# Values of the last 16 tokens: plain fp32 products in four column groups in place of tiles of three products

## The reference

```python
h = jnp.concatenate([meta, x], axis=1)              # 16 + 512 = 528 tokens
xn = rms_norm(h, norm_gains[layer, 0])
proj = xn @ w_in[layer]                             # 528 x 1024 times 1024 x PROJ_WIDTH, fp32
q_a, k_a, v_a, f_a, q_b, k_b, v_b, g_a, g_b = jnp.split(proj, SPLIT_POINTS, axis=-1)
log_f = jax.nn.log_sigmoid((f_a + b_forget[layer]).astype(jnp.float32))
o_a = forgetting_attention(_split_heads(q_a, 8), _split_heads(k_a, 8), _split_heads(v_a, 8),
                           log_f.transpose(0, 2, 1))
o_b = stick_breaking_attention(_split_heads(q_b, 8), _split_heads(k_b, 8), _split_heads(v_b, 8))
y_a = _merge_heads(o_a) @ w_o_fox[layer]            # then gates, w_out, the FFN and a second block
```

## Time and profile before

| | value |
|---|---|
| median of 3 runs | 1541.97 us |
| profiled execution, its own time | 1542.34 us |
| its span (first to last instruction) | 1540.5 us |
| PE busy | 1492.9 us, 97% of the span |
| PEld busy | 1319.4 us, 86% |
| DVE busy | 1025.0 us, 67% |
| ACT busy | 655.0 us, 43% |
| mean granted TensorE clock | 0.993 |
| loads of 1 MB on SP's queue, issue to landing, median | 4.8 us |

### The profile page before, as it was taken

One profiled execution on the slowest core, in us unless ns is written; L12 is line 12 of the kernel. 1 busy time (PEld: TensorE's weight loads), 2 busy tenths in 40 slices (PEclk: granted clock), 3 DMA queues, 4 the chain that ended last, 5 costly groups with the idle time before them and its releaser, 6 DMA issues.

```text
span 1540.5 us, 27902 instructions
## 1 busy us (share of the span) xinstructions
PE 1492.9 (97%) x11772; PEld 1319.4 (86%) x11772; DVE 1025.0 (67%) x1441; ACT 655.0 (43%) x1052; POOL 23.3 (2%) x20
## 2 busy tenths in 40 slices
PE   7999999999998999999999899999989999999998
PEld 7989878889998999999777667768667999998876
DVE  5533447875446977777665766676688888885454
ACT  5433443443334222212343555446645555554343
POOL 0000000000000000000000011000000000000000
PEclk9999999999998999999999999999999999999999
DMA  5222004443222323322344213110113233222222
GB/s 183 83 83 83 16 21 161 148 160 109 105 101 74 115 103 120 121 103 101 133 149 150 92 50 110 55 35 29 35 48 110 83 110 110 106 94 79 93 96 82
DMA packets 37707, 147.74 MB, mean 96 GB/s; under 512 B 4304, under 2 KB 4432, under 8 KB 27856
## 3 DMA queue, kind: packets, MB, share of 16 engines
q1 hardware_dynamic: 36288, 142.76, 26.8%
q10 hardware_dynamic: 1152, 2.16, 0.4%
q0 software_dynamic: 144, 1.05, 0.2%
HBM read 143.86 MB, written 2.10 MB: 95 GB/s over the span
## 4 chain that ended last, share of the span: by engine, by line
PE 83%; DVE 9%; ACT 5%; issue 2%; DMA 1%; POOL 0%; ACTq 0%; DVEq 0%
PE ps L567 19%; PE ps L569 18%; PE ps L568 18%; PE ps L1488 4%; PE ps L1486 4%; PE ps L1487 4%; ACT t L1539 2%; DVE t L2264 1%; PE ps L603 1%; PE ps L604 1%; PE ps L605 1%; PE ps L751 1%; PE ps L1192 1%; PE ps L729 1%; PE ps L1161 1%
## 5 line engine op out<-in xcount | busy, mean ns | idle before, releaser
L567 PE MATMUL ps<-t 128*128 128x258 f32 (+4 forms) x2160 | 689.0, 319 | 21.9 <-DVE t L2312 8.6
L569 PE MATMUL ps<-t 128*128 128x258 f32 (+4 forms) x2160 | 677.4, 314 | 0.0
L568 PE MATMUL ps<-t 128*128 128x258 f32 (+4 forms) x2160 | 676.2, 313 | 0.0
L567 PEld LDWEIGHTS ps<-t 128*128 128x128 f32 (+1 forms) x2160 | 407.6, 189 | 66.0 <-issue 16.0
L569 PEld LDWEIGHTS ps<-t 128*128 128x128 f32 (+1 forms) x2160 | 407.3, 189 | 27.2
L568 PEld LDWEIGHTS ps<-t 128*128 128x128 f32 (+1 forms) x2160 | 408.3, 189 | 23.8
L2264 DVE TENSOR_TENSOR t<-t 128x1024 fp32r<-128x1024 f32 (+2 forms) x121 | 205.8, 1700 | 203.8 <-ACT t L1539 203.8
L1539 ACT ACTIVATE t<-t 128x1024 fp32r<-128x1024 f32 (+2 forms) x121 | 174.0, 1438 | 186.0 <-PE ps L569 173.4
L1488 PE MATMUL ps<-t 128*128 128x256 f32 x504 | 142.6, 283 | 0.0
L1486 PE MATMUL ps<-t 128*128 128x256 f32 x504 | 142.5, 283 | 0.1
L1487 PE MATMUL ps<-t 128*128 128x256 f32 x504 | 141.3, 280 | 0.0
(11 more groups left out here) (322 smaller groups left out, 1771.5 us busy)
## 6 DMA issues: line engine op xcount, KB each, us to landing
t<-in_W SPq DMA_DIRECT2D x75, 1024.0 KB, 4.8
t<-in_W SPq DMA_DIRECT2D x62, 512.0 KB, 3.2
t<-in_W SPq DMA_DIRECT2D x100, 256.0 KB, 3.5
t<-in_W SPq DMA_DIRECT2D x4, 644.0 KB, 3.8
t<-in_XT ACTq DMA_DIRECT2D x8, 264.0 KB, 7.8
out<-t SPq DMA_DIRECT2D x8, 256.0 KB, 2.7
t<-in_ROPE POOLq DMA_DIRECT2D x1, 1024.0 KB, 5.3
t<-in_CONS SPq DMA_DIRECT2D x1, 423.0 KB, 11.7
```

Source lines behind the costliest of these rows:

```text
L567: pe.matmul(out, wh, xh, start=first, stop=False)
L568: pe.matmul(out, wh, xl, start=False, stop=False)
L569: return pe.matmul(out, wl, xh, start=False, stop=last)
```

## The change

The last 16 tokens' values leave the tiles of three. For each pair of chunks (va 0 and 1, vb 0 and 1) one step `v_ends` makes all 512 columns with plain fp32 matmuls from the raw weights in `wraw`: for each of 8 contraction blocks four matmuls of 128 columns, each into another group of 32 PSUM partitions (rows 0, 32, 64, 96; 16 rows used) of bank 0. That is 32 matmuls with a 128x16 stationary operand instead of 2 x 24 matmuls of 256 columns. The stationary operand `xend` is a new fp32 tile, high plus low of those tokens, made by one DVE addition. DVE copies the result out with four copies of 16x128 instead of two of 16x256.

`v_ends` needs both raw chunks of the pair at once, so it stands fifth of nine steps: tiles 0 to 3 of the first chunk, `v_ends`, tiles 0 to 3 of the second. SP's loads into the two slots now also wait for it (`RAW_USED`): qb 0 and qb 1 wait for va's, ga 0 and woa 0 for vb's. `FILL_A` has a filler less of vb, and fills the place by cutting the first qb tile into its two parts, steps 0 and 1; the others come a step later. vb's `v_ends` is in step 13, and vb 1's first tile, with ga 0's split, in step 14.

```diff
@@ tables @@
-                   ("mm_v", 5, [("va", 0), ("va", 1), ("vb", 0), ("vb", 1)]),
+for _i, _c in enumerate(("va", "vb")):
+    USED[_c, 0], USED[_c, 1] = ("mm_v", 9 * _i + 4), ("mm_v", 9 * _i + 9)
+RAW_USED = {(_c, _i): 9 * _p + 5 for _p, _c in enumerate(("va", "vb")) for _i in range(2)}
-FILL_A = [("qb", 0, 0), ("qb", 0, 1), ("qb", 1, 0), ("qb", 1, 1), ("kb", 0, 0), ("kb", 0, 1), ("kb", 1, 0), ("kb", 1, 1)]
-FILL_A += [("vb", _i, _t) for _i in range(2) for _t in range(5)]
+FILL_A = [("qb", 0, 0, (0,)), ("qb", 0, 0, (1,)), ("qb", 0, 1, (0, 1)), ("qb", 1, 0, (0, 1)), ("qb", 1, 1, (0, 1))]
+FILL_A += [("kb", _c, _i, (0, 1)) for _c in range(2) for _i in range(2)]
+FILL_A += [("vb", 0 if _at < 5 else 1, _at, ()) for _at in range(9)]
+def chunk_starts(f):
+    name, c, i, parts = FILL_A[f]
+    return i in (0, 5) if name == "vb" else i == 0 and parts[0] == 0
@@ build @@
+        xend = sb(s_fox, [P, 8, 16])
@@ SP, weights @@
+                if n >= 2 and ORDER[n - 2] in RAW_USED:
+                    sp_.wait_ge(S["mm_v"], RAW_USED[ORDER[n - 2]])
@@ PE @@
-            for c in range(2):
-                w = weights(AT["va", c], 8)
-                for t in range(5):
-                    v_tile(c, t, w, min(128, T1 - 128 * t), 2 * c if t % 2 else 0,
-                           0 if t % 2 else (3 * c + 1 if t == 4 else 3 * c))
+            def v_ends(name):
+                pe.wait_ge(S["f_d"], 1)
+                for n in (AT[name, 0], AT[name, 1]):
+                    pe.wait_ge(S[f"d_w{n % 2}"], 16 * (n // 2 + 1))
+                for k in range(8):
+                    for g in range(4):
+                        at = 256 * k + 128 * (g % 2)
+                        ins = pe.matmul(bank(0, 128, slice(32 * g, 32 * g + 16)), xend[:, k, :],
+                                        wraw[:, AT[name, g // 2] % 2, at:at + 128], start=(k == 0), stop=(k == 7),
+                                        skip_group_check=True)
+                ins.then_inc(S["mm_v"], 1)
+            def v_step(pair, i):
+                nonlocal w
+                name = ("va", "vb")[pair]
+                if i in (0, 5):
+                    w = weights(AT[name, i // 5], 8)
+                if i >= 4:
+                    e = i - 4
+                    pe.wait_ge(S["ev_v_a" if e % 2 else "ev_v_d"], 4 * pair + e // 2 + 1 if e % 2 else
+                               6 * pair + (1, 2, 4)[e // 2])
+                if i == 4:
+                    v_ends(name)
+                else:
+                    tokens(w, i - i // 5 * 5, T1, P, i % 4).then_inc(S["mm_v"], 1)
+            for i in range(9):
+                v_step(0, i)
@@ ACT (DVE alike: split at i == 5, evac_v by steps) @@
-            for c in range(2):
-                split(AT["va", c] + 1)
-                for t in range(5):
-                    evac_v(c, t)
+            split(AT["va", 0] + 1)
+            for i in range(9):
+                if i == 5:
+                    split(AT["va", 1] + 1)
+                evac_v(0, i)
@@ DVE @@
+            dv.wait_ge(S["xl"], 16)
+            dv.tensor_tensor(xend[:, :, :], xnh[:, :, T2:T1].bitcast(F), xnl[:, :, T2:T1].bitcast(F), ALU.add
+                             ).then_inc(S["f_d"], 1)
+                if i == 4:
+                    for g in range(4):
+                        ins = dv.tensor_copy(dst[0:16, 4, 128 * g:128 * g + 128], bank(0, 128, slice(32 * g, 32 * g + 16)))
+                        if g % 2:
+                            ins.then_inc(S["ev_v_d"], 1)
...
```

More of the change, by code:

```diff
@@ L182, with qk_of @@
 XH0 = (8, 16, 32, 40)
-FILL_A = [("qb", 0, 0), ("qb", 0, 1), ("qb", 1, 0), ("qb", 1, 1), ("kb", 0, 0), ("kb", 0, 1), ("kb", 1, 0), ("kb", 1, 1)]
-FILL_A += [("vb", _i, _t) for _i in range(2) for _t in range(5)]
+FILL_A = [("qb", 0, 0, (0,)), ("qb", 0, 0, (1,)), ("qb", 0, 1, (0, 1)), ("qb", 1, 0, (0, 1)), ("qb", 1, 1, (0, 1))]
[4 more added lines that the diff above has]
+    return i in (0, 5) if name == "vb" else i == 0 and parts[0] == 0
+def qk_of(f):
+    name, c, i, _ = FILL_A[f]
+    return (8 if name == "qb" else 12) + 2 * c + i
 def evac_b(f):
@@ L660, in _, with qk_tile @@
                         ins.then_inc(S["mm_qk"], 1)
-            def qk_tile(g, w):
+            def qk_tile(g, w, parts=(0, 1)):
                 if g < 8:
@@ L669, in qk_tile @@
                         pe.wait_ge(S["ev_qk_a"] if g % 2 else S["ev_qk_d"], g // 2 - 4 if g % 2 else 4 + g // 2)
-                    tile(w, g % 2, 128, 8, xnh, xnl, 0, H2, 2 * (g % 2)).then_inc(S["mm_qk"], 1)
+                    for q in parts:
+                        ins = tile(w, g % 2, 128, 8, xnh, xnl, 264 * q, H2[q:q + 1], 2 * (g % 2) + q)
+                    if 1 in parts:
+                        ins.then_inc(S["mm_qk"], 1)
             w = weights(1, 8)
@@ L708, in fox_scores @@
                     pe.wait_ge(S["ev_qk_d"], 8)
-                    pe.wait_ge(S["f_d"], 3)
+                    pe.wait_ge(S["f_d"], 4)
                     pe.wait_ge(S["cst"], 9)
@@ L792, in fill_a @@
                 nonlocal w
-                name, c, i = FILL_A[f]
-                if i == 0:
-                    w = weights(AT[name, c], 8)
[L796 to L806, removed]
+                name, c, i, parts = FILL_A[f]
+                if name == "vb":
+                    if i == 0:
+                        pe.wait_ge(S["ev_qk_d"], 12)
+                    if i == 2:
+                        pe.wait_ge(S["ev_qk_a"], 4)
+                    v_step(1, i)
+                    return
+                if chunk_starts(f):
+                    w = weights(AT[name, c], 8)
+                if f == 0:
+                    pe.wait_ge(S["ev_v_d"], 6)
+                    pe.wait_ge(S["ev_v_a"], 4)
+                qk_tile(qk_of(f), w, parts)
             for n in range(20):
@@ L1638, in evac_qk, with evac_v @@
                               ).then_inc(S["ev_qk_a"], 1)
-            def evac_v(c, t):
-                if t % 2 == 0:
+            def evac_v(pair, i):
+                if i % 2 == 0:
                     return
[L1644 to L1647, removed]
+                t, col = i - i // 5 * 5, 256 * (i // 5)
+                ac.wait_ge(S["mm_v"], 9 * pair + i + 1)
+                ac.activation((va, vb)[pair][:, t, col:col + 256], bank(i % 4, 256), ACT.Copy).then_inc(S["ev_v_a"], 1)
             split(AT["f", 0] + 1)
@@ L1661, in _ @@
             ac.wait_ge(S["cst"], 1)
-            ac.wait_ge(S["f_d"], 2)
+            ac.wait_ge(S["f_d"], 3)
             ac.activation(ct[0:8, :], cs, ACT.Copy).then_inc(S["f_a"], 1)
-            for c in range(2):
-                split(AT["va", c] + 1)
-                for t in range(5):
-                    evac_v(c, t)
+            split(AT["va", 0] + 1)
[3 more added lines that the diff above has]
+                evac_v(0, i)
             def fox_exp(n):
@@ L1707, in fill_a @@
             def fill_a(f, part):
-                name, c, i = FILL_A[f]
+                name, c, i, parts = FILL_A[f]
                 if part == 0:
-                    if i == 0:
+                    if chunk_starts(f):
                         split(AT[name, c] + 1)
                 elif name == "vb":
-                    evac_v(2 + c, i)
-                else:
-                    evac_qk(8 + f)
+                    evac_v(1, i)
+                elif 1 in parts:
+                    evac_qk(qk_of(f))
             for n in range(20):
@@ L2332, in norm0, with evac_v @@
                 norm_tiles(0, 0, T1, lambda k: h[:, k, :], lambda k: V("g0", k), None, xnh, xnl, k0, k1)
-            def evac_v(c, t):
-                if t % 2:
+            def evac_v(pair, i):
+                if i % 2:
                     return
-                dst, col, m = (va, 256 * c, min(P, T1 - 128 * t)) if c < 2 else (vb, 256 * (c - 2), min(P, T1 - 128 * t))
-                dv.wait_ge(S["mm_v"], 5 * c + t + 1)
-                dv.tensor_copy(dst[0:m, t, col:col + 256], bank(t % 4, 256, slice(0, m))).then_inc(S["ev_v_d"], 1)
+                dst, t, col = (va, vb)[pair], i - i // 5 * 5, 256 * (i // 5)
+                dv.wait_ge(S["mm_v"], 9 * pair + i + 1)
+                if i == 4:
[3 more added lines that the diff above has]
+                            ins.then_inc(S["ev_v_d"], 1)
+                else:
+                    dv.tensor_copy(dst[:, t, col:col + 256], bank(i % 4, 256)).then_inc(S["ev_v_d"], 1)
             dv.wait_ge(S["rst"], 1)
@@ L2359, in _ @@
                                     ).then_inc(S["f_d"], 1)
-            dv.wait_ge(S["f_d"], 1)
+            dv.wait_ge(S["f_d"], 2)
             dv.tensor_tensor_scan(cs, cf, cf, 0.0, ALU.add, ALU.bypass).then_inc(S["f_d"], 1)
@@ L2409, in fill_a @@
             def fill_a(f, part):
-                name, c, i = FILL_A[f]
+                name, c, i, parts = FILL_A[f]
                 if part == 0:
-                    if i == 0:
+                    if chunk_starts(f):
                         split(AT[name, c] + 1)
```

(6 more changed lines are left out.)

6 lines of the change are left out of this document (removed).

## The result

The changed kernel takes 1537.79 us in the median of 6 runs (1535.6 to 1538.13), before 1542.12 beside it (6 runs, 1541.25 to 1542.56). The ratio is 0.9971 with an interval of 0.9961 to 0.9982: 4.3 us less, where 6.35 were forecast. The profiled execution took 1538.07 us, its span is 1536.3.

A forecast was written before the change was run, and what follows sets the result against it. PE, busy for 97% of the span, was taken to bound the kernel. 4.55 us from the va stretch plus 1.8 from the fox loop, 6.35 in all, gave 1535.6 us as median, range 1533.2 to 1539.8.

The forecast's parts named there:

- likeliest case: `v_ends` runs four abreast, with new waits between 0 and 3 us; 1533.7 to 1537, chance 0.73.
- What goes: 16-token tiles cost as much as full ones: two of 5.6 us in va, two fillers of 5.94 in the fox loop.
- the va stretch: PE from the first va tile to the first fox scores, 29.45 us: 4.55 us go, qb 0's load stays covered.
- `v_ends`: 32 plain fp32 matmuls on PE, four abreast: 2.05 us each time with switches, in va and in fox step 13.
- fox scores row: Trace of four 512-column matmuls, each in its own column group: 0.22 us a set of four at 128 columns.
- two abreast: Rival: 128 rows feed no more than two streams, `v_ends` takes 4.0 us; 1538.9 in all, chance 0.12.
- one after the other: Slower rival: `v_ends`' column groups run serially, 7.6 us each time; 1546.1 in all, chance 0.05.
- The fox loop: Two fillers out, one `v_ends` and a switch in: 3.7 us less 1.9 of new waits gives 1.8.
- sum of waits: New PE waits in fox steps 13 and 14: 0.45, 0.2, 0.95 and 0.3, together 1.9 us.
- Everything behind is only moved: All after the fox loop keeps its length and comes some 6.4 us earlier.
- The late load: Rival: ga 0's load lands beyond 4.7 us, delaying step 14; 1538.9 at 8 us, 1542.6 at 11.7; chance 0.08.
- none of the new waits: Rival: the close races in steps 13 and 14 cause no waits; 1533.7; no chance of its own given.

The follow-up runs named there:

- e_vb_only: Against the kernel before: `v_ends` for vb alone, va's tiles as before; 1540.92 us, ratio 0.9995.
- e_late_split: Against the changed kernel: the split of ga 0 on ACT and DVE moved from step 14 to step 15; 1535.35 us.
- e_vb_early: Against the changed kernel: vb's `v_ends` in the third of its nine places, fox step 11 instead of 13; 1534.28 us, run again 1535.70.
- the repeat: The changed kernel run once more, unaltered; 1537.88 us, ratio 0.9974 to the kernel before.
- e_two_groups: Against the changed kernel: `v_ends` writes to two column groups and two halves of each instead of four groups; 1542.70 us.
- e_one_group: Against the changed kernel: `v_ends` writes all four quarters to one column group, at four offsets in the bank; 1549.64 us.

## Why the prediction was right, and where it was not

**The direction, the mechanism and the range held.** 1537.8 lies in 1533.2 to 1539.8, faster by 0.29%. It is above the likeliest case's own range (1533.7 to 1537).

**What goes, and the va stretch: right.** 4.55 us forecast, 4.53 measured, and the stretch took 24.90 to 24.93 us in the six other kernels that have it unchanged. The wait behind the fifth tile went, nothing took its place, and qb 0's load stayed covered.

**`v_ends`: right, slightly dear.** 2.05 forecast, 1.87 measured. The bound that decided it was the fox scores row, a set of four at 0.22 us. The bounds of two abreast (4.0) and one after the other (7.6) were measured at 3.6 and 7.1. The rule from the Trainium skill, TensorE: Matmul & The Clock Gate (What overlaps and what doesn't), that weight loads overlap with running matmuls only where the row group differs, does not hold here: 32 matmuls with the same row group and their own loads run at a quarter of the serial time. The same page (Measured speedup vs the span model) has 2.38 for three column groups at 512 columns, 0.79 for each; here it is 3.8 for four at 128 columns, 0.95 for each.

**The fox loop: right in kind, 0.74 us too good.** 1.8 forecast, 1.06 measured, and e_vb_only had the same. All four waits were named, with their causes; e_late_split and e_vb_early removed two and four of them and got 1.27 and 2.44 us. The mis-sized term is the sum of waits, 1.9 for 2.5. As idle time the four are 0.48, 0.50, 0.79 and 0.28, in all 2.05: the sum was nearly met, with the second too small (I took the four DVE copies 0.2 us apart, they are 0.3 apart) and the third, the load's, too large. The other 0.5 is what I had at nothing: from start to start each wait costs 0.07 to 0.17 us more than its idle time. The rest of the loop's difference, some 0.3 us less 0.2 for the shorter `v_ends`, I did not take apart.

**"Everything behind is only moved": wrong by about 1 us.** This is the step that failed, and no rival held it. The start was 0.67 us later in the profiled run; as the ten other profiles, that of before among them, have it at 65.6 to 66.3, I take it for chance. The tail was 0.72 longer and in the repeat 2.9: its first part 1.0 and 2.7, with the gap in PE's issue. The stages alone would have given 1536.5; the median stayed at 1537.8 in two sets of runs. Why PE stops there stays open.

**The rivals.** Two abreast would have been 1538.9 and one after the other 1546.1; those kernels took 1542.7 and 1549.6. So the slower rival would have been a real loss. The late load did not come: 4.8 us from issue to split, where its row said 4.7. With none of the new waits it would have been 1533.7; all four were there, and the kernel that has none of them, e_vb_early, took 1534.3 and 1535.7. In the rivals' sums I let the load's wait stand as it was, which e_two_groups shows to be wrong. That is 1.1 us of its 3.8; most of the others lie in the tail, 2.6 us longer than before in its profile.

## What to carry to other kernels

A narrow stationary operand costs as much as a full one (0.117 us a matmul with 16 columns of it, 0.118 with 128); the moving columns are paid. Where the rest of a product is narrow, here 16 rows, column groups with plain fp32 can undercut three rounded products: 1.87 us for 5.6 with four groups, 3.6 with two, and with one it is a loss. When a filler is made shorter, give it a step with a short chain, and look at every load that it now holds back: it should be issued at least a landing and a split ahead of its use, here 4.8 and 1.9 us. A change is worth the sum of its stages only if the rest stays as it was; compare the stages by themselves, since a median of the whole can hide a microsecond either way.

## What the runs showed that I had not expected

PE can stand still for 0.8 to 1.1 us in the midst of its own matmuls, with nothing in the profile that it waits for: in six of eleven profiles, always behind the 26th of the same 32 tiny matmuls. Behind the gap of 1.1 us the granted clock fell to the 1.2 GHz level for some 3 us; the tail's first part was then 1.8 us longer than with a gap of 0.8, where the clock stayed at 2.4 GHz.

In e_one_group the same came behind the wait of 1.98 us in step 14. PE was busy for 2.0 of the 4 us up to 208, and the clock was at 1.2 GHz from 209 to 212:

```profile
204.00:208.00 4.00, 2.02 (x22) 1.30 (x21) 2.46 (x3) 2.75 (x7) 0.00 (x0) 1.00 0.03 13
209.00:212.00 3.00, 3.00 (x15) 3.00 (x16) 0.91 (x3) 1.70 (x6) 0.00 (x0) 0.50 0.00 0
214.00:218.00 4.00, 4.00 (x35) 3.16 (x32) 1.94 (x3) 1.27 (x4) 0.00 (x0) 1.00 0.01 4
```

The matmuls there come 15 in 3 us, at half the pace, so about 1.4 us were lost on top of the wait: the loop's 6.6 us more are 5.2 of `v_ends`, 1.2 of the longer load wait and 1.4 of clock, less 1.2 of covered waits.
